# Two transformer blocks on one core: the layers' attention with outputs computed already turned, logits negated, probabilities scaled before their turn, and three probability buffers

## The reference, cut to what matters

```python
def mla_mixer(...):                     # 8 heads, causal, "M" below
    s = (qn @ k_nope + qr @ k_rope) * scale
    p = masked_softmax(s, kpos <= qpos)
    o = p @ v                           # 256 x 512
def nsa_mixer(...):                     # 8 heads, three branches
    p_c = masked_softmax(q @ kc - slopes * dist)      # "K": 15 compressed keys
    p_s = masked_softmax(q @ k_slc - slopes * dist)   # "S": selected keys
    p_w = masked_softmax(q @ k_win - slopes * dist)   # "W": window keys
    o = g0 * (p_c @ vc) + g1 * (p_s @ vs) + g2 * (p_w @ vw)   # 256 x 512
mix = concatenate([o_a, o_b], -1) @ w_out
x = layer_norm(ALPHA * x + mix)
xa: softmax(q @ k_mem) @ v_mem, 4 heads of 256        # "X"
```

## Time and profile before

| | us |
|---|---|
| median of three runs | 1697.3 |
| the profiled execution, its own time | 1696.81 |
| its span, first to last instruction | 1694.9 |
| TensorE busy in the span | 1665.5 (98%) |
| VectorE busy | 1223.2 (72%) |
| ScalarE busy | 352.5 (21%) |
| GpSimd busy | 212.7 (13%) |
| chain that ended last, share on TensorE | 90% |
| the same, share on VectorE | 5% |

### The profile page before, as it was taken

One profiled execution on the slowest core, in us unless ns is written; L12 is line 12 of the kernel. 1 busy time (PEld: TensorE's weight loads), 2 busy tenths in 40 slices (PEclk: granted clock), 3 DMA queues, 4 the chain that ended last, 5 costly groups with the idle time before them and its releaser, 6 DMA issues.

```text
span 1694.9 us, 22817 instructions
## 1 busy us (share of the span) xinstructions
PE 1665.5 (98%) x8726; PEld 1281.4 (76%) x8726; DVE 1223.2 (72%) x2230; ACT 352.5 (21%) x893; POOL 212.7 (13%) x139
## 2 busy tenths in 40 slices
PE   7999999999999999999999999999999999999998
PEld 6887488877847886477784969994687767699953
DVE  6777467976787777573376778996844685789995
ACT  2111000034511111112270212220012531222210
POOL 1222211121021212211001000002120000000021
PEclk9999999999999999999999999999999999999999
DMA  9685454524176555346513536444447206265440
GB/s 320 194 230 177 146 199 162 175 80 149 51 232 213 160 164 184 124 145 178 207 51 131 155 125 194 156 170 153 158 121 252 100 1 224 71 226 177 150 173 25
DMA packets 163755, 267.07 MB, mean 158 GB/s; under 512 B 4279, under 2 KB 106477, under 8 KB 163519
## 3 DMA queue, kind: packets, MB, share of 16 engines
q1 hardware_dynamic: 157902, 248.66, 43.8%
q0 software_dynamic: 5008, 15.91, 3.3%
q10 hardware_dynamic: 736, 1.05, 0.3%
HBM read 262.52 MB, written 2.03 MB: 156 GB/s over the span
## 4 chain that ended last, share of the span: by engine, by line
PE 90%; DVE 5%; DVEq 2%; issue 1%; ACT 1%; DMA 1%; SPq 0%; ACTq 0%
PE psum L1017 19%; PE psum L886 16%; PE psum L1065 13%; PE psum L952 12%; PE psum L844 7%; PE psum L1275 4%; PE psum L1481 3%; PE psum L1538 3%; PE psum L1190 3%; PE psum L1116 3%; PE psum L1232 2%; PE psum L825 2%; PE psum L1104 2%; PE psum L1206 1%; PE psum L1221 1%
## 5 line engine op out<-in xcount | busy, mean ns | idle before, releaser
L695 POOL TENSOR_TENSOR work<-ring,work 128x1024 f32<-128x1024 f32 (+2 forms) x59 | 147.4, 2499 | 791.5 <-DVE work L2199 791.5
L2191 DVE TENSOR_TENSOR work<-ring 128x1024 f32<-128x1024 f32 (+2 forms) x102 | 122.0, 1196 | 83.3 <-PE psum L1065 74.3
L1065 PE MATMUL psum<-ring,work 128*128 128x512 f32 x352 | 160.8, 592 | 0.0
L2195 DVE TENSOR_TENSOR ring<-ring 128x1024 f32<-128x1024 f32 (+2 forms) x104 | 131.7, 1267 | 7.7
L2199 DVE TENSOR_TENSOR work<-ring 128x1024 f32<-128x1024 f32 (+2 forms) x102 | 122.6, 1202 | 7.6
L1065 PEld LDWEIGHTS psum<-ring,work 128*128 128x128 f32 x352 | 66.4, 190 | 81.1 <-issue 79.9
L1065 PE MATMUL psum<-work 128*128 128x512 f32 x264 | 122.5, 592 | 0.0
L1017 PE MATMUL psum<-x_t,work 128*128 128x128 f32 x832 | 101.4, 275 | 0.0
L1017 PE MATMUL psum<-work,ring 128*128 128x128 f32 x832 | 101.4, 275 | 0.0
L1017 PE MATMUL psum<-x_t,ring 128*128 128x128 f32 x832 | 97.4, 275 | 1.6 <-ACT x_t L1610 1.6
L1017 PEld LDWEIGHTS psum<-x_t,work 128*128 128x128 f32 x832 | 97.1, 192 | 0.0
(11 more groups left out here) (304 smaller groups left out, 2865.6 us busy)
## 6 DMA issues: line engine op xcount, KB each, us to landing
ring<-in_ffn_w_up_dram SPq DMA_DIRECT2D x66, 1024.0 KB, 7.9
ring<-in_w_in_dram SPq DMA_DIRECT2D x21, 2048.0 KB, 7.9
ring<-in_ffn_w_down_dram SPq DMA_DIRECT2D x20, 2048.0 KB, 7.8
ring<-in_ffn_w_gate_dram SPq DMA_DIRECT2D x22, 1024.0 KB, 5.7
ring<-in_xa_wkv_dram SPq DMA_DIRECT2D x8, 2048.0 KB, 9.5
ring<-in_w_out_dram SPq DMA_DIRECT2D x6, 2048.0 KB, 10.9
ring<-in_xa_wq_dram SPq DMA_DIRECT2D x4, 2048.0 KB, 7.9
ring<-in_xa_wo_dram SPq DMA_DIRECT2D x4, 2048.0 KB, 11.3
```

Of the source, the lines that this page charges most:

```text
L695: nc.gpsimd.tensor_tensor(t4, quarters(n, chunks, pitch)[2], t2, ALU.subtract).then_inc(fourth_ready, 1)
L1065: last = mm(sums[p], acts[p][:, q, :], rhs[:, i, :], start=(q == 0), stop=(q == KF // 2 - 1))
L2191: v.tensor_tensor(t3, b22, b12, ALU.subtract)
L2195: v.tensor_tensor(b12, b12, b11, ALU.subtract)
```

## The change

Only the layers' attention (units K, S, W, M) and, in small parts, X are changed.

- `value` is computed turned: the stationary operand is the 64 columns of v, the moving one the 128 columns of turned probabilities. Head 0 of a pair goes to PSUM partitions 0 to 63, head 1 to 64 to 127. All nine K, S and W units of a tile accumulate in one region of PO, the four M units in the other. Values of an S unit are computed with those of its W, those of an even M with the odd one, so one group of matmuls covers two units.
- As the branches are summed in PSUM, each unit's probabilities are scaled before their turn: VectorE's mid multiplies them by reciprocal and gate (line 2437 of the new kernel), with one instruction of 128 or 256 columns per head. It stands right behind the next unit's logits. `output` is gone for these units.
- Logits are negated in the instruction that adds the bias (scale -1, minimum in place of maximum), so its accumulated result is NM itself and the small negation goes; exp gets scale -1. This holds for X too.
- ScalarE copies the four finished regions of PO (nine units' or four units' worth) straight to XT, in turned_rows_out; turn_mixed and its transposes are gone.
- The turn lags by three units in place of two (ahead=3), with four logits buffers and three probability buffers.
- K of tile 1 moves from the second place of the list to the fourteenth, at the start of tile 1.

```diff
-UNITS_2 = [unit("K", 0, i) for i in range(TT)] + \
-          [x for i in range(TT) for x in [unit(k, h, i) for h in range(4) for k in "SW"] + [unit("M", h, i) for h in range(4)]]
+UNITS_2 = [x for i in range(TT) for x in
+           [unit("K", 0, i)] + [unit(k, h, i) for h in range(4) for k in "SW"] + [unit("M", h, i) for h in range(4)]]
...
+                    for t in (j - 1, j):
+                        y = units[t]
+                        o = (512 if k == "M" else 0) + P * y["n"]
+                        for kb in range(y["nk"]):
+                            for s in range(2):
+                                n = s * y["nk"] + kb
+                                last = mm(PO[HD * s:HD * s + HD, o:o + P], values(y, s, kb), pts(y, u0 + t)[:, n * P:(n + 1) * P],
...
-                    if 0 <= j - 2 < n:
-                        turn(j - 2)
+                    if 0 <= j - ahead < n:
+                        turn(j - ahead)
...
-                    if 0 <= j - 3:
-                        value(j - 3)
+                    if 0 <= j - ahead - 1:
+                        value(j - ahead - 1)
...
-                shared_product(L_OUT, F_LOUT + F_LAYER * l, A_LOUT + A_LAYER * l, E_O, turn_mixed(E_O, U1 + TT + 12, 19, l), l)
+                shared_product(L_OUT, F_LOUT + F_LAYER * l, A_LOUT + A_LAYER * l, "O", lambda i: None, l)
...
+                    if 0 <= j - ahead - 1 < n and units[j - ahead - 1]["kind"] in "WM" and units[j - ahead - 1]["n"] == 3:
+                        turned_rows_out(j - ahead - 1)
...
+                            if x["kind"] in "SWMX":
+                                last = v.tensor_tensor_reduce(out=dst, in0=src, in1=bias_of(x, s), scale=-1.0, scalar=-TAKEN,
+                                                              op0=ALU.add, op1=ALU.min, accum_out=NM[:, b4, s:s + 1])
...
+                    if x["kind"] in "SW":
+                        c = 3 * 2 * x["n"] + (1 if x["kind"] == "S" else 2)
+                        for s in range(2):
+                            last = v.tensor_scalar(L[:, s * n:(s + 1) * n], L[:, s * n:(s + 1) * n], RC[:, b4, s:s + 1],
+                                                   ngate[:, x["tile"], c + 3 * s:c + 3 * s + 1], ALU.mult, ALU.mult)
```

More of the change, by code:

```diff
@@ L1178, in values, with attend @@
                 return KV[:, kb, c:c + HD]
-            def attend(units, u0, l=None, between={}, behind_turn={}):
+            def attend(units, u0, l=None, between={}, behind_turn={}, ahead=2):
                 def scores(j):
@@ L1235, in attend @@
                 n = len(units)
-                for j in range(n + 3):
+                for j in range(n + ahead + 1):
                     if j in between:
@@ L1555, in _ @@
                 pe.wait_ge(key_shift, at(32, 32, l))
-                attend(UNITS_2, U1, l, {1 + 2 * i + h: values_between(i, h) for i in range(TT) for h in range(2)})
+                attend(UNITS_2, U1, l, {1 + 2 * i + h: values_between(i, h) for i in range(TT) for h in range(2)}, ahead=3)
                 pe.wait_ge(group_free, at(H_WV + 2, G_LAYER, l))
-                shared_product(L_OUT, F_LOUT + F_LAYER * l, A_LOUT + A_LAYER * l, E_O, turn_mixed(E_O, U1 + TT + 12, 19, l), l)
+                shared_product(L_OUT, F_LOUT + F_LAYER * l, A_LOUT + A_LAYER * l, "O", lambda i: None, l)
                 pe.wait_ge(share_in, 4 * l + 4)
@@ L1676, in first_copies, with attend @@
                 hidden(UPS - 1)
-            def attend(units, u0, l=None, between={}, behind_copy={}):
+            def attend(units, u0, l=None, between={}, behind_copy={}, ahead=2):
                 def exps(j):
@@ L1691, in exps @@
                             v = L[:, s * n:(s + 1) * n]
-                            last = activation(v, v, ACT.Exp, bias=NM[:, b4, s:s + 1], accum_out=SM[:, b4, s:s + 1])
+                            last = activation(v, v, ACT.Exp, scale=-1.0 if x["kind"] in "SWMX" else 1.0, bias=NM[:, b4, s:s + 1],
+                                              accum_out=SM[:, b4, s:s + 1])
                         last.then_inc(probs_ready, 1)
@@ L1714, in mixed_rows, with turned_rows_out @@
                         copy(dst, src).then_inc(unit_done, 1)
+                def turned_rows_out(j):
+                    x, u = units[j], u0 + j
+                    act.wait_ge(values_ready, at(u + 1, U2, l))
+                    i, sparse = x["tile"], x["kind"] == "W"
+                    src = PO[:, 0:512] if sparse else PO[:, 512:1024]
+                    src = src.rearrange("p (k t) -> p k t", k=4)
+                    dst = XT[:, 4:8, i * P:(i + 1) * P] if sparse else XT[:, 0:4, i * P:(i + 1) * P]
+                    if not sparse and i == 0:
+                        copy(dst[:, 0:2, :], src[:, 0:2, :]).then_inc(quarter_out, 1)
+                        copy(dst[:, 2:4, :], src[:, 2:4, :]).then_inc(unit_done, TILE_UNITS - SPARSE_UNITS)
+                    else:
+                        copy(dst, src).then_inc(unit_done, SPARSE_UNITS if sparse else TILE_UNITS - SPARSE_UNITS)
                 n = len(units)
-                for j in range(n + 4):
+                for j in range(n + ahead + 2):
                     if j in between:
                         between[j]()
-                    if 0 <= j - 2 < n:
-                        out_of_psum(j - 2)
+                    if 0 <= j - ahead < n:
+                        out_of_psum(j - ahead)
                     if j in behind_copy:
@@ L2320, in bias_of, with attend @@
                 return zero_bias[:, 0:x["keys"]]
-            def attend(units, u0, l=None, between={}, mid_first=None):
+            def attend(units, u0, l=None, between={}, mid_first=None, ahead=2):
                 def logits(j):
@@ L2327, in logits @@
                     dve.wait_ge(scores_ready, at(u + 1, U2, l))
[L2328 to L2329 removed]
+                    if j > ahead:
+                        dve.wait_ge(probs_turned, at(u - ahead, U2, l))
                     o = b * 1024
@@ L2789, in _ @@
                     weight_sums(F_LOUT + F_LAYER * l + d, 4, D)
-                attend(UNITS_2, U1, l)
+                attend(UNITS_2, U1, l, ahead=3)
                 both_tiles()
```

115 lines of the change are left out of this document (64 added, 51 removed).

## The result

The changed kernel takes 1684.4 us in the median of 6 runs (1684.2 to 1684.7); the kernel before, beside it, takes 1696.9 (1696.5 to 1697.4, 6 runs). The ratio is 0.9926, with a 95% interval of 0.9914 to 0.9938: 12.5 us less. The forecast was 1687.4 with a range of 1681.5 to 1695.5, so direction and range hold, and the gain was 2.7 us larger than forecast (9.8), by over a quarter.

The account below looks back on a forecast made before the run. TensorE, busy 98% at full clock, bounds the kernel, with VectorE pacing tile 0. Per layer 2.7 + 2.6 - 0.8 - 1.9 + 2.04 + 0.3 = 4.9 us, two layers 9.8, giving 1687.4 us; range 1681.5 to 1695.5.

Parts of the forecast that it names:

- (a): Values in two column halves: records 0.054 us apart, 0.27 us per excursion; a tile 1 unit's value 0.57 instead of 0.84.
- (b): Tile 1's pace: TensorE stays the bound at 1.92 us a unit instead of 2.19; gain 2.7 us a layer.
- (c): Tile 0's pace: 1.20 us a unit instead of 1.52 over about eight uncovered iterations; gain 2.6 us a layer.
- (d): K of tile 1 in the middle: TensorE waits 0.8 us at K's turn, a loss in each layer.
- (e): End of a layer's attention: waits of 0.45, 1.05 and 0.9 us; 5.45 us against 3.51, a loss of 1.9.
- (f): Transposes of O1 after the last values go: 2.04 us of TensorE saved a layer, VectorE's sums costed at nothing.
- (g): X units: the negation leaves a chain on which TensorE starts; gain 2 x 0.16 = 0.3 us a layer.
- No overlap: Rival, in value: the 64-column groups run one after the other at 0.107 us; 1698.5 us, chance 0.10.
- drains at each change between halves: Rival, in value: 72 changes between halves a layer drain at 0.17 us each; 1722 us, chance 0.05.
- handovers: Rival: handovers between three engines set the pace, tile 1 at 2.05 us, tile 0 at 1.32; 1695.5 us, chance 0.13.
- No gaps: Rival: K and the end cost nothing, absorbed by the look-ahead; 7.6 us a layer, 1682 us, chance 0.12.

## Why the prediction was right, and where its sizes were off

*(a) Two halves at once: right.* Forecast 0.054 a record, taken from rows with four groups of 32 partitions; measured 0.0537. With one half only it is 0.107, so this term is shown, not argued. The price of an excursion was forecast at 0.27 and measured at 0.34, or 0.37 in a group of 16. What the overlap is worth can't be given as a share of the 12.5 us: taken away alone, the overlap costs 11.0 us, the folded negation 6.9 and the third unit of distance 15.1, together far more than the gain, so the parts can't be added. The half in the theory above is no share that a run shows. The move of K, the fourth logits buffer and the two small output scalings that went were not tested alone.

*(b) Tile 1: right.* Forecast 1.92 a unit, measured 1.91, with two small errors against each other (the price of the excursion 0.05 a unit too low, scores and turn 0.05 too high).

*(c) Tile 0: the mis-sized term.* VectorE's unit was forecast at 1.13 and is 1.06 with one pointer and 1.18 with two, 1.14 in the mean of a tile's eight S and W and four M units. Two errors cancel there: the negation is worth 0.24 and not 0.16, and a pair of scalings with two pointers costs 0.52 and not 0.40. The 0.07 for handing over, taken for caution, is not there: from the scores at 849.35 to those at 858.50 eight units take 1.14 each, against 1.20; that holds for layer 0, while layer 1 loses 0.36 of it in the open wait shown above. How the first stretch of the table came to 3.57 instead of 2.34 can be told from the starts of scores, as both kernels have scored equally many units by the fifth place of the list (before, K of tile 1 in place of one of tile 0) and the same units by the fourteenth:

| stretch, by the start of scores | before | after | of it K's of tile 1, moved |
|---|---|---|---|
| first scores to unit 5 (850.84; 849.35) | 19.73 | 18.23 | -1.24 |
| unit 5 to unit 14 (863.78; 859.67) | 12.94 | 10.32 | +0.37 |
| unit 14 to unit 18 (870.91; 867.35) | 7.13 | 7.68 | +0.90 |

K's own work comes to the same (0.37 by which its scores are longer than a unit's, and its values of 0.9). Without it the nine iterations of tile 0 gain 12.94 - 9.95 = 2.99, 0.33 each, where 8 x 0.32 = 2.6 was forecast: the first of them were quicker than 1.52 before (1.44 in the mean of the nine), which takes back what the handing over gives, and one iteration more is uncovered than was counted. The four about the change of tiles gain 7.13 - 6.34 = 0.79 when the wait of 0.44 at K is set apart too, where 0.54 was forecast. The first stretch is shorter by 0.26, of which 0.22 is one turn of tile 0: with the turn three units behind, one turn fewer stands in front. The forecast counted the third turn behind the last scores as a loss and forgot that it is missing here. With K's wait that makes 0.4 + 0.25 + 0.26 + 0.36 = 1.27 of more gain, against 1.23 in the table.

*(d) K: right in place, too large.* One wait of TensorE at the turn of K, as forecast, but 0.44 in place of 0.8 (0.60 from start to start; counted so, 0.16 of what is here put down to K belongs to the iterations about it, and the sum stays):

```profile
859.70 0.27 DVE L2379 MEMSET work<- 128x256 f32 x1 [0.26 <-PE psum L1196]
...
862.28 0.28 DVE L2419 TENSOR_TENSOR work<-work,shared 128x120 f32<-128x120 f32 x1
```

```profile
864.09 0.44 PE L1212 MATMUL psum<-ident_fours,work 128*128 128x128 f32 x2 [0.44 <-DVE work L2429]
```

In VectorE's timeline its logits stand from 859.70 and its mid from 862.28; the next logits follow at 863.95, 1.67 later (forecast 1.75). VectorE even waited 0.26 in front of K's logits, so it came to K with nothing left over from the units before, against the prediction's sign that it has no gap there.

*(e) The end: right.* Forecast three waits of 0.45, 1.05 and 0.9; there are two, 0.73 and 0.68, and no wait for the turn of 24. From start to start they are 0.96 and 0.89, entering included, so 1.85 in place of 2.4. But the two groups take 1.02 each and not 0.86, since they pay for leaving, 0.33 together. The loss is 1.70 where 1.94 was forecast. The cause of the second wait was only half seen: the copy follows the last turn in this order, and in any other order the buffer's old tenant holds it.

*(f) Transposes: right.* 2.04 a layer. The cover held: VectorE's sums begin at 889.53 (its first instruction from x_t), 1.8 us behind the product's start, and the 16 records of the product stand without a gap from 887.75 to 894.72.

*(g) X: right, 0.23 once* in place of 0.16 twice, as TensorE waits for this chain at the first unit only.

*The rivals.* No overlap fell with the experiment in one half. Two terms of its sum were off and nearly cancel: by the prediction's own rows a unit of tile 1 would take 2.34 and not 2.32 (2.35 was measured in that experiment), and one of tile 0 1.32 and not 1.36; drains at each change between halves fell with 0.054 a record (its case is the one without overlap, which alone is slower than before, so it would have spoken against the change from any price on, not from 0.02 us); handovers did not set the pace, since both tiles of layer 0 run at what one engine needs by itself (tile 1 at TensorE's 1.91, tile 0 at VectorE's 1.14), but for the 0.30 before the first group. No gaps, 1682, was nearest in time (2.4 us off against 3.0 for the forecast) but for another reason: its gaps at K and at the end are there, with 0.44, 0.73 and 0.68. The steps that failed are sizes, nearly all in the first stretch: the count of iterations in (c), the 0.8 of (d), and a turn counted at the end and not taken off at the start. They explain layer 0, 6.5 us where 4.9 was forecast; that layer 1 gains 0.4 less and that 0.3 are lost behind the last memory product the forecast did not have, and what VectorE stood on there is open.

## What to carry to other kernels

Matmuls with 64 output partitions run two at once if their outputs lie in different column halves; bundle them, because each excursion from full width has a price (here 0.34 us, six records' worth). A small instruction that needs an accumulated result costs, beside its own time, the drain that the code puts in front of it (here 0.24 us together), so fold it into the instruction that accumulates. When a reordering moves a wait and doesn't shorten it, look for the second thing that the waiting instruction needs, here the buffer of three units ago, and take both away in one run.

## What was not expected of the hardware

- The scores behind an excursion take 0.10 us more until their turn can start (0.97 against 0.87), beside entering (0.10) and leaving (0.17).
- The overlap of the halves doesn't need alternation: with four records in a row per half a group of 16 takes 1.08 in place of 1.03.
- A scaling with two pointers, and so two multiplications, is slower than one with one, 0.26 against 0.20 us for 128 columns; which of the two differences costs it no run shows.
- A negation of 128x2 elements, for which the profile shows 0.17, was worth 0.24 us on VectorE in the kernel before, 0.23 in the changed one and 0.23 in X, the drain in front of it included.
